# Triangular inverse on 32x32 diagonal blocks with two joining levels, and products of one tile shape put together, in a hybrid streaming encoder

## The reference, cut to what matters

```python
def gdn_chunk(S, q, k, v, g, beta):
    ...
    a_low = jnp.where(strict, jnp.einsum('bhik,bhjk->bhij', kb, k) * lmask, 0.0)
    m = a_low + jnp.eye(L, dtype=jnp.float32)
    rhs = jnp.concatenate([v * beta[..., None], kb * jnp.exp(decay)[..., None]], axis=-1)
    sol = lax.linalg.triangular_solve(m, rhs, left_side=True, lower=True, unit_diagonal=True)
    val, kcd = sol[..., :DV_A], sol[..., DV_A:]
    v_new = val - jnp.einsum('bhlk,bhkv->bhlv', kcd, S)
    attn = jnp.einsum('bhik,bhjk->bhij', q, k) * lmask
    o = (jnp.einsum('bhlk,bhkv->bhlv', q * jnp.exp(decay)[..., None], S)
         + jnp.einsum('bhij,bhjv->bhiv', attn, v_new))
    ...

def ret_chunk(R, q, k, v, lg):
    ...
    inner = jnp.einsum('bhij,bhjv->bhiv', jnp.einsum('bhik,bhjk->bhij', q, k) * dmask, v)
    cross = jnp.einsum('bhlk,bhkv->bhlv', q * jnp.exp(lg[:, None] * (n + 1.0))[..., None], R)
    ...
    return R_new, inner + cross
```

## Time and profile before

| | us |
|---|---|
| median of 3 runs | 1453.14 (1452.51 to 1454.01) |
| the profiled execution's own time | 1451.69 |
| its span in the profile | 1449.9 |
| PE busy in the span | 1410.7 (97%) |
| DVE busy | 827.2 (57%) |
| ACT busy | 630.4 (43%) |
| POOL busy | 146.3 (10%) |

### The profile page before, as it was taken

How to read it: one execution, slowest core, us unless ns; L and a number is a source line. 1 busy time by engine, 2 the same in 40 slices (tenths; PEclk the granted TensorE clock), 3 DMA queues, 4 the chain that set the end, 5 groups by cost and what they waited for, 6 DMA issues and landing times.

```text
span 1449.9 us, 25140 instructions
## 1 busy us (share of the span) xinstructions
PE 1410.7 (97%) x10482; PEld 1365.7 (94%) x10482; DVE 827.2 (57%) x986; ACT 630.4 (43%) x755; POOL 146.3 (10%) x183
## 2 busy tenths in 40 slices
PE   5999999999999899999999999999999989999997
PEld 4999999998888899999999999999988879999997
DVE  4655544788755455554455554459777455555532
ACT  4433333556435443333343333446543454333333
POOL 2200001213001200000120000113200021000010
PEclk9999999999999999999999999999999999999999
DMA  6744445644011354444555444555321123454442
GB/s 186 234 145 148 134 140 147 180 138 133 21 42 63 105 173 145 145 124 141 170 180 193 145 136 122 157 166 160 117 78 59 59 78 119 152 156 143 120 140 77
DMA packets 228298, 191.09 MB, mean 132 GB/s; under 512 B 4077, under 2 KB 225686, under 8 KB 228086
## 3 DMA queue, kind: packets, MB, share of 16 engines
q1 hardware_dynamic: 225360, 181.94, 41.4%
q0 software_dynamic: 2416, 7.75, 1.6%
q10 hardware_dynamic: 438, 0.25, 0.1%
HBM read 185.91 MB, written 5.59 MB: 132 GB/s over the span
## 4 chain that ended last, share of the span: by engine, by line
PE 94%; DVE 2%; ACT 2%; issue 1%; DMA 0%; ACTq 0%; DVEq 0%
PE psum L672 22%; PE psum L673 22%; PE psum L674 21%; PE psum L784 5%; PE psum L785 5%; PE psum L786 5%; PE psum L739 2%; PE psum L734 2%; PE psum L886 1%; DVE wlo L1382 1%; PE psum L891 1%; PE psum L875 1%; ACT whi L1052 1%; PE psum L829 1%; PE psum L801 1%
## 5 line engine op out<-in xcount | busy, mean ns | idle before, releaser
L1052 ACT ACTIVATE whi<-raw 128x2048 fp32r<-128x2048 f32 (+1 forms) x158 | 268.3, 1698 | 535.3 <-PE psum L674 534.9
L1382 DVE TENSOR_TENSOR wlo<-raw,whi 128x2048 fp32r<-128x2048 f32 (+1 forms) x158 | 319.9, 2025 | 250.6 <-ACT whi L1052 250.5
L672 PE MATMUL psum<-hh,whi 128*128 128x320 f32 x1408 | 437.0, 310 | 4.7 <-issue 4.4
L673 PE MATMUL psum<-hl,whi 128*128 128x320 f32 x1408 | 436.2, 310 | 0.0
L674 PE MATMUL psum<-hh,wlo 128*128 128x320 f32 x1408 | 436.2, 310 | 0.0
L672 PEld LDWEIGHTS psum<-hh,whi 128*128 128x128 f32 x1408 | 265.4, 189 | 6.0 <-issue 5.9
L673 PEld LDWEIGHTS psum<-hl,whi 128*128 128x128 f32 x1408 | 265.3, 188 | 0.2
L674 PEld LDWEIGHTS psum<-hh,wlo 128*128 128x128 f32 x1408 | 265.3, 188 | 0.0
L672 PE MATMUL psum<-act_hi,whi 128*128 128x320 f32 x704 | 217.9, 309 | 0.0
L674 PE MATMUL psum<-act_hi,wlo 128*128 128x320 f32 x704 | 217.4, 309 | 0.0
L673 PE MATMUL psum<-act_lo,whi 128*128 128x320 f32 x704 | 217.4, 309 | 0.0
(11 more groups left out here) (294 smaller groups left out, 1532.7 us busy)
## 6 DMA issues: line engine op xcount, KB each, us to landing
raw<-in_w_ffn_gate SPq DMA_DIRECT2D x44, 1024.0 KB, 5.4
raw<-in_w_ffn_up SPq DMA_DIRECT2D x44, 1024.0 KB, 5.4
raw<-in_w_ffn_down SPq DMA_DIRECT2D x64, 704.0 KB, 4.6
raw<-in_w_in SPq DMA_DIRECT2D x30, 1024.0 KB, 5.4
raw<-in_w_out SPq DMA_DIRECT2D x8, 1024.0 KB, 5.3
bias_copies<-bias_row POOLq DMA_DIRECT2D x2, 768.0 KB, 6.9
cst<-in_consts POOLq DMA_DIRECT2D x1, 1190.0 KB, 8.2
tok<-in_x_prompt SPq DMA_DIRECT2D x2, 512.0 KB, 5.2
```

The source lines that it names most:

```text
L672: pe.matmul(out, wh, hi[:, k0 + k, :], start=start and k == 0, stop=False)
L673: pe.matmul(out, wh, lo[:, slot[k] if slot else k0 + k, :], start=False, stop=False)
L1052: ins = A(whi[:, u % SPLIT, 0:n], raw[:, u % RAW, 0:n], ACT.Copy)
L1382: V.tensor_tensor(wlo[:, s, 0:n], raw[:, u % RAW, 0:n], whi[:, s, 0:n].bitcast(F32), ALU.subtract).then_inc(lo_done, 1)
```

## The change

**Blocks of 32.** `T1`, `Y` and `Z` of the levels 2 to 16 run on 32x32 diagonal blocks, so there are four products a head on a tile of 128 positions (two on the tile of 64), each of 32 rows, 32 columns and 32 moving columns, where there were two (one) of 64. The masks, `Wt`, `Wn` and `Ysb` shrink to 32 columns a head. Level 32 becomes a joining level like level 64: `Y` and `Z` work on pairs of blocks (32x32 products again), and ACT, no longer DVE, drains both, into `Vt` and, for level 64, into a 64x64 block `joined`. On the tile of 64 positions `Vt` now exists too and level 32 is its last. ACT's `as` copies four (two) blocks into `Vt` and two into `joined`, and POOL clears `Vt` and `joined` ahead of the gate spreads (`ug`).

**Products of one shape together.** In `o` and `oC` the four state products come first and the four products of the current tile behind them.

**The tables.** All four tables are written in another order; the level-32 drains move from DVE's table to ACT's.

```diff
-HB = 64
+HB, QB = 64, 32
...
-vn:0 Z:2:4 oB:3 ctok:0 cqk:0 Y:2:8 Y:1:32 R:0 oC:0 ctok:1 cqk:1 Z:2:8 Su:0 QK:0 Y:2:16 Z:1:32 part:14:1 Y:1:64
+Y:2:8 QK:0 cqk:0 Z:2:8 Y:0:16 QK:1 Z:0:16 Y:2:16 Z:1:8 oC:0 ctok:1 Y:0:32 Y:1:16 part:15:1 Z:0:32 Z:1:16 Z:2:16
...
                     elif kind == "T1":
...
-                            for r in halves(L):
-                                mm = pe.matmul(bank[r, h * HB:(h + 1) * HB], Wt[r, h, :], C("block_ident")[r, :],
+                            for r in quarters(L):
+                                mm = pe.matmul(bank[r, h * QB:(h + 1) * QB], Wt[r, h, :], C("block_ident")[r, :],
                                                start=True, stop=True)
...
+                        if s == HB:
+                            pe.wait_ge(*S("assembled", RANK["as", t]))
                         for h in range(H):
...
-                            for r in halves(L):
-                                mm = pe.matmul(bank[r, cols], U[r, h, r], Wn[r, h, :], start=True, stop=True)
+                                mm = pe.matmul(bank[HB:P, cols], U[0:HB, h, HB:P], joined(Vn)[:, h, :], start=True, stop=True)
+                            elif s == QB:
+                                for r, low in pairs_of(L):
+                                    mm = pe.matmul(bank[low, cols], U[r, h, low], Wn[r, h, :], start=True, stop=True)
+                            else:
+                                for r in quarters(L):
+                                    mm = pe.matmul(bank[r, cols], U[r, h, r], Wn[r, h, :], start=True, stop=True)
...
+                        elif s == QB:
+                            for h in range(H):
+                                for r, low in pairs_of(L):
+                                    mm = pe.matmul(bank[r, h * QB:(h + 1) * QB], Y32[low, h, :], Wt[low, h, :],
+                                                   start=True, stop=True)
+                            if t < 2:
+                                low = slice(QB, HB)
+                                for h in range(H):
+                                    mm = pe.matmul(bank[low, (H + h) * QB:(H + h + 1) * QB], Wt[low, h, :], Y32[low, h, :],
+                                                   start=True, stop=True)
+                        else:
+                            for h in range(H):
+                                for r in quarters(L):
+                                    mm = pe.matmul(bank[r, h * QB:(h + 1) * QB], Y32[r, h, :], Wt[r, h, :],
+                                                   start=True, stop=True)
...
+                        if t:
+                            for h in range(H):
+                                pe.matmul(bank[:, h * L:(h + 1) * L], state[:, h, :], q(h), start=h == 0, stop=False)
                         for h in range(H):
-                            if t:
-                                pe.matmul(bank[:, h * L:(h + 1) * L], state[:, h, :], q(h), start=True, stop=False)
                             mm = pe.matmul(bank[:, h * L:(h + 1) * L], vn[0:L, h, :], aT[0:L, h, 0:L],
-                                           start=t == 0, stop=True)
+                                           start=t == 0, stop=t == 0 or h == H - 1)
...
+                    elif kind == "z":
+                        key = ("Z", t, QB)
+                        wait_filled(act, key)
+                        if t < 2:
+                            low = slice(QB, HB)
+                            me.do(A(joined(Vn)[low, :, 0:QB], compact(small(key)[low], 1), ACT.Copy, scale=-1.0))
+                        for r, low in pairs_of(L):
+                            ins = A(Vt[r, :, low], compact(small(key)[r]), ACT.Copy, scale=-1.0)
+                            me.drain(ins, key) if low.stop == L else me.do(ins)
                     elif kind == "as":
-                        wait_drained(act, ("Z", t, HB // 2))
-                        Wt, _ = both(Vn, L)
-                        for n, r in enumerate(halves(L)):
-                            me.do(A(Vt[r, :, r], Wt[r, :, :], ACT.Copy), "assembled" if n else None)
+                        wait_drained(act, ("Z", t, QB // 2))
+                        act.wait_ge(*S("spread", RANK["ug", t]))
+                        for r in quarters(L):
+                            if t < 2 and r.stop <= HB:
+                                me.do(A(joined(Vn)[r, :, r], Wn[r, :, :], ACT.Copy))
+                            me.do(A(Vt[r, :, r], Wt[r, :, :], ACT.Copy), "assembled" if r.stop == L else None)
```

More of the change, by code:

```diff
@@ L94 @@
 PE_WORK = work("""
[L95 to L99, removed]
@@ L111 @@
[L111 to L115, removed]
@@ L325, in both, with joined, quarters @@
         def both(Vn, L):
-            v = Vn.rearrange("p h l -> p (h l)").rearrange("p (a h l) -> p a h l", a=2, h=H)
+            v = square(Vn, 0, DEC).rearrange("p h l -> p (h l)").rearrange("p (a h l) -> p a h l", a=2, h=H)
             return v[0:L, 0], v[0:L, 1]
-        def halves(L):
-            return [slice(HB * c, HB * c + HB) for c in range(L // HB)]
+        def joined(Vn):
+            return square(Vn, H * DEC, DEC)[0:HB]
+        def quarters(L):
+            return [slice(QB * c, QB * c + QB) for c in range(L // QB)]
         vn_of = [B[0]["U"], B[0]["U"], square(B[1]["U"])]
@@ L459, in in_turn, with pairs_of @@
                 body(n, 0)
+        def pairs_of(L):
+            return [(slice(HB * a, HB * a + QB), slice(HB * a + QB, HB * a + HB)) for a in range(L // HB)]
         def convs_done(i):
@@ L879, in _ @@
                         wait_drained(pe, ("Y", t, s))
-                        for h in range(H):
-                            cols = slice(h * HB, (h + 1) * HB)
-                            if s == HB:
-                                mm = pe.matmul(bank[0:HB, cols], Ysb[HB:P, h, 0:HB], Wt[HB:P, h, :], start=True, stop=True)
-                                continue
-                            for r in halves(L):
-                                mm = pe.matmul(bank[r, cols], Ysb[r, h, 0:HB], Wt[r, h, :], start=True, stop=True)
@@ L995, in _ @@
                             pe.wait_ge(state_loaded, (layer + 1) * 32)
+                        out = lambda b, r: bank[r, b * P:b * P + L]
+                        if t:
+                            for h in range(H):
+                                b, r = h // 2, slice(64 * (h % 2), 64 * (h % 2) + 64)
+                                pe.matmul(out(b, r), rstate[r, b, :], bq[r, b, c0:c0 + L], start=b == 0, stop=False)
                         for h in range(H):
                             b, r = h // 2, slice(64 * (h % 2), 64 * (h % 2) + 64)
-                            out = bank[r, b * P:b * P + L]
-                            if t:
-                                pe.matmul(out, rstate[r, b, :], bq[r, b, c0:c0 + L], start=True, stop=False)
-                            mm = pe.matmul(out, ctv[:, 64 * h:64 * h + 64], aC[:, h, 0:L], start=t == 0, stop=True)
+                            mm = pe.matmul(out(b, r), ctv[:, 64 * h:64 * h + 64], aC[:, h, 0:L], start=t == 0,
+                                           stop=t == 0 or b == 1)
                         fill(mm, step)
@@ L1587, in _ @@
                         wait_filled(dve, key)
-                        me.drain(V.tensor_tensor(Ysb[0:L, :, 0:HB], flat(small(key)[0:L]), blocks(f"below{s}", slice(0, L)),
-                                                 ALU.mult), key)
+                        me.drain(V.tensor_tensor(square(Ysb, 0, QB)[0:L], compact(small(key)[0:L]),
+                                                 blocks(f"below{s}", slice(0, L)), ALU.mult), key)
                     elif kind == "z":
```

107 lines of the change are left out of this document (64 added, 43 removed).

## The result

| | us |
|---|---|
| before, median of 6 runs | 1452.84 (1452.06 to 1454.9) |
| the changed kernel, median of 6 runs | 1445.67 (1439.12 to 1447.98) |
| ratio, with its 95% interval | 0.994 (0.9925 to 0.9955) |
| the profiled execution | 1439.12, its span 1437.3 |
| predicted | 1434.0 (1424 to 1448) |

The changed kernel is faster, as forecast, but by 7 us in the median where 19 were forecast. The time lies inside the range. Its runs lie 9 us apart where those of before lie 3 apart, and they go with the mean granted clock: 1439.1 and 1440.4 us at 0.991, 1445.2 and 1446.6 at 0.985 and 0.986, 1446.1 at 0.984, 1448.0 at 0.982. The profiled run of before was at 0.993.

A forecast was written before the change was run, and what follows sets the result against it. PE, busy for 97% of the span, bounds the kernel. Per layer -8.7 + 1.4 - 3.9 + 1.6 = -9.6, twice -19.2: 1451.7 to 1432.5, plus 1.4 for the median: 1434 us, range 1424 to 1448.

The forecast's parts named there:

- Part two: In o and oC, grouping products of one shape saves 3.9 us per layer.
- The price of a turn: In the inverse, four 32x32 tiles run records side by side in 37 ns; blocks of 32 save 8.7 us per layer.
- The flat turn: Rival: in the inverse, 32 columns still take 58 ns as 64 do; 1448 us, chance 0.08.
- the floor of 25 ns: Rival: any two PE records start at least 25 ns apart; 4.3 us lost per layer, 1462 us, chance 0.04.
- changes of shape in part one: Blocks of 32 add 10 switches of PE tile shape per layer, 0.14 us each: 1.4 us more.
- New waits: PE's added waiting in the mixing stage, allowed at today's 0.9 + 0.7: 1.6 us more per layer.
- waits over 4 us a layer: Sign: PE's waits in the mixing stage should stay under 4 us a layer.
- The clock: PE's full clock, read in the mixing stage before, was kept for the change; no term in the sum.
- ACT at the joins: Rival: ACT's 22 more small copies in the inverse, 6.2 us per layer, delay PE; 1443 us, chance 0.20.
- The third rival: PE's queue hands out at most two records in 58 ns; 8.7 us lost per layer, 1470 us, chance 0.08.
- PE idles behind vn:0: Sign against the forecast: PE waiting in the mixing stage after vn:0, where only one dense part remains.
- four tiles do not share a turn: Sign against the forecast: in the inverse, 32x32 records on four tiles would not run side by side.

The follow-up runs named there:

- e1_part_two: The kernel before with only the new order of the products in o and oC: 1445.62 us, ratio 0.9944.
- e2_part_one: The changed kernel with the old order of the products in o and oC put back: 1449.16 us, ratio 0.9979.
- e4_again: The changed kernel without any edit, in a later series of runs: 1441.91 us, ratio 0.9915.
- e6_burst: The changed kernel plus 1024 constant records per layer, 64x64 pairs in the first, four 32x32 tiles in the second: added stretches 30.0 and 26.3 us.
- e8_mixed: The changed kernel with two weight loads and a store issued later and dense parts spread among the inverse's small steps: 1436.59 us, ratio 0.9902.

## Why the prediction was right and wrong

**Part two: right.** It was worth 6.5 us in e1_part_two and 7.2 between e2_part_one and e4_again, where 7.8 were forecast. The parts in the trace of after, against the earlier trace rows: oC of tile 1 takes 1.07 us (forecast 1.1), oC of tile 2 0.76 (0.75), o of tile 2 1.87 (2.0):

```profile
437.04 0.65 PE L1027 MATMUL psum<-bq,pR 64*64 64x128 f32 x8
...
438.11 0.40 PE L1038 MATMUL psum<-cv,ck 128*64 128x64 f32 x8
...
445.17 0.45 PE L1027 MATMUL psum<-bq,sR 64*64 64x64 f32 x8
...
445.93 0.44 PE L749 MATMUL psum<-cst,qkv 128*128 128x128 f32 x2
...
453.53 1.00 PE L942 MATMUL psum<-qkv,sS 128*128 128x64 f32 x8
...
455.40 0.44 PE L744 MATMUL psum<-U,kt 64*128 64x128 f32 x2
```

**The price of a turn: right.** Four tiles do share a turn. At full clock, a Z step of tile 0 and one of tile 1 follow each other, 0.61 us for 16 turns or 38 ns:

```profile
370.15 0.45 PE L914 MATMUL psum<-Vn,tmp 32*32 32x32 f32 x32
...
370.76 0.42 PE L914 MATMUL psum<-Vn,Ysb 32*32 32x32 f32 x29
```

And e6_burst's block takes 1.09 us for 32 turns, 34 ns. Forecast was 37, from the earlier trace rows, a single row in which three records start together. The flat turn and the floor of 25 ns are out. The 1.4 us for the changes of shape in part one no run has by itself.

**"New waits", 1.6 us a layer: wrong, and the first of two terms that failed.** The step was "I go through the table and find other tiles' work ahead of nearly every wait". It looked for waits on engines. The waits that came hang on no engine: 4.7 us a layer on the supply of instructions, beside 1.4 on DVE and ACT, 6.1 in all. Before's whole lists, with the 0.4 of "issue" and the 0.3 on POOL that the earlier trace rows leave out, add up to 2.3 and 1.9. So the two layers wait 8.0 us more than before where the sum had 3.2 more: 4.8 too little. The sign that the prediction gave, waits over 4 us a layer, came.

**The clock: put at nothing, and the second.** The prediction read the full clock in the earlier trace rows and kept it for the new order, without a reason. In the profiled run the inverse has 6.8 us at half clock in each layer, in which PE is busy 6.0 and 6.3 us: some 3 us of work lost a layer, 6.1 together. Behind the end of the stage, where before is at half clock too, PE works 2.8 and 2.9 us at half clock instead of 3.1 and 4.1: some 0.8 us back. 1432.5 + 4.8 + 6.1 - 0.8 = 1442.6, against 1439.1 measured. So the two terms more than cover the 6.6 us that the profiled run is over the forecast; which of the sizes is 3.5 us too large, no run tells. The other runs have lower clocks, and so more of the second term: from 0.991 to 0.985 is 0.006 x 1440 = 9 us at most, and 6 were measured. This is the gap between the profiled run and the median of 1445.7. What brings the clock down at a given place stays open.

**The range.** That 1445.7 lies in it is luck: its high end stood for ACT at the joins and for flat turns, and neither came.

**The rivals.** ACT at the joins: refuted; no wait on a copy into `Vt` or `Vn` stands in the list of after, and the list's ACT row is the 0.6 us of `btv`. Its 1443 is near the median for another reason. The third rival, two records in 58 ns, named the number that counts: 29 to 31 ns a record is what the 32x32 products of e6_burst take over their whole run. It named the wrong place for it. PE and its queue do hand out four records in 34 ns; it is the blocks of instructions behind them that come at that rate. The kernel before sat just at it with its 58 ns turns, and its trace shows a single such wait, of 0.4 us; so I took 29 ns for a matter of tiles. That the kernel did not go to 1470 I put down to the order: a step of the inverse is shorter than a block, and dense parts lie between; where two or three steps stand in a row, the block behind them is late. The spread order of e8_mixed bears this out.

**What was to show it wrong** was "if PE idles behind vn:0". It idles ahead of it, in T1, in the levels up to 16 and in the retention steps among them. The other sign, that four tiles do not share a turn, did not come.

## What to carry to other kernels

Count instructions as well as time: where a stretch takes up PE instructions faster than some 256 in 3.5 to 4 us for more than a block or two, look in the trace of the faster version for "issue" waits in the midst of steps. Where they stand, a shorter matmul no longer helped here; dense work between the small steps, and no big transfer just ahead, kept most of it hidden here. An engine that bounds the kernel can also lose its clock by the change that speeds it up, as 32x32 products did here where 64x64 pairs kept it. So compare the mean granted clock of several runs before a time is believed, and put a range on a forecast that rests on full clock.

## What the runs showed of the hardware

- PE took up 1024 records and their weight loads at 29 ns a record in 64x64 pairs without a wait, and at 29 to 31 ns on four 32x32 tiles with a pause at each 256th instruction, though within the first blocks, at full clock, a record takes 8.5 ns.
- 32x32 products on a single tile, with PE busy without a gap, lost the full clock 4.5 us into their run and did not get it back in the 46.5 us to its end; 64x64 pairs kept it for 28.
- Stores of 640 KB beside a weight load delayed a 16 KB instruction transfer: it started 4.4 us after PE had entered a block, against 0.3 to 1.8 us for the next three. With the stores alone moved the pause behind it went.
